# Moving the gating of the mixed rows from the gate stage into the output stage of a hybrid encoder

## The reference

```python
p = h @ w_in
..., q_mem, gate = jnp.split(p, ...)
o_mix = mla_mixer(...)            # layer 0: softmax attention; layer 1: sgu_mixer
o_mem = memory_attention(q_mem, mem, ...)
o = jnp.concatenate([o_mix, o_mem], axis=-1) * jax.nn.silu(gate)
x = x + o @ w_out[i]
```

## Time and profile before

| what | us |
|---|---|
| median of three runs | 3594.59 |
| the profiled execution, its own time | 3603.56 |
| its span, first to last instruction | 3601.5 |
| PE busy | 3326.9 (92%) |
| DVE busy | 2006.2 (56%) |
| ACT busy | 1581.8 (44%) |
| POOL busy | 1389.1 (39%) |

### The profile page before, as it was taken

The page is one execution under the profiler, slowest core; times in us unless marked ns, Lnnn a source line. Parts: engine busy times, 40 slices in busy tenths (PEclk is TensorE's granted clock), DMA queues, the critical chain, the costliest instruction groups (busy, mean ns, idle before and its releaser), DMA issues. The chain is left out here.

```text
span 3601.5 us, 46116 instructions
## 1 busy us (share of the span) xinstructions
PE 3326.9 (92%) x16108; PEld 2735.6 (76%) x16108; DVE 2006.2 (56%) x3007; ACT 1581.8 (44%) x2396; POOL 1389.1 (39%) x914
## 2 busy tenths in 40 slices
PE   8969959999999999999697998997999959799899
PEld 8968837777777777777496887885888849688787
DVE  4457758888888888888376332113333337522211
ACT  4446627777777777777454121003222225412100
POOL 1148828888888888888410000000000011000000
PEclk9979969999999999999898999998999969799999
DMA  7769980222222221221354996554222244488555
GB/s 279 260 225 314 306 233 18 66 67 61 67 62 65 52 56 44 67 61 22 115 174 129 290 292 217 197 175 177 88 91 103 90 180 165 131 259 242 175 189 173
DMA packets 454870, 537.91 MB, mean 149 GB/s; under 512 B 55609, under 2 KB 372409, under 8 KB 434993
## 3 DMA queue, kind: packets, MB, share of 16 engines
q1 hardware_dynamic: 454704, 535.81, 48.5%
HBM read 324.98 MB, written 210.61 MB: 149 GB/s over the span
## 5 line engine op out<-in xcount | busy, mean ns | idle before, releaser
L1235 POOL TENSOR_TENSOR at_acc<-at_acc,at_ph 128x1024 f32<-128x1024 f32 x288 | 690.9, 2399 | 79.0 <-ACT at_ph L1161 58.2
L1269 DVE TENSOR_TENSOR at_pl<-at_sc,at_ph 128x1024 fp32r<-128x1024 f32 x408 | 498.6, 1222 | 139.3 <-ACT at_sc L1162 139.0
L1161 ACT ACTIVATE at_ph<-at_sc 128x1024 fp32r<-128x1024 f32 x408 | 418.5, 1026 | 336.2 <-PE at_sc L1081 336.1
L1255 DVE TENSOR_REDUCE at_mx<-at_mxp 128x1 f32<-128x512 f32 x816 | 522.2, 681 | 26.7 <-PE at_mxp L1092 25.0
L1162 ACT ACTIVATE at_sc<-at_sc 128x1024 f32<-128x1024 f32 x408 | 416.3, 1020 | 0.0
L1077 PE MATMUL at_sc<-at_qt,at_kt 97*128 97x512 f32 x816 | 331.4, 406 | 12.5 <-DMA at_qt<-at_neg 9.7
L1079 PE MATMUL at_sc<-at_qt,at_kt 96*128 96x512 f32 x816 | 326.0, 399 | 0.0
L1106 PE MATMUL at_o_hi<-at_ph,at_v 128*128 128x512 f32 x816 | 322.4, 395 | 2.1 <-DVE at_half L1274 2.1
L1081 PE MATMUL at_sc<-at_qt,at_kt 96*128 96x512 f32 x816 | 323.7, 397 | 0.0
L1108 PE MATMUL at_o_lo<-at_pl,at_v 128*97 128x512 f32 x816 | 321.8, 394 | 0.0
L1092 PE MATMUL at_mxp<-at_kt,at_qt 96*128 96x512 f32 x816 | 276.8, 412 | 25.2 <-DMA at_kt<-kT 20.4
(11 more groups left out here) (246 smaller groups left out, 7350.5 us busy)
## 6 DMA issues: line engine op xcount, KB each, us to landing
ma_h<-hT SPq DMA_DIRECT2D x40, 1024.0 KB, 4.8
ogT<-ga_st SPq DMA_DIRECT2D x160, 256.0 KB, 3.5
ou_o<-ogT SPq DMA_DIRECT2D x40, 1024.0 KB, 6.1
ga_h<-hT SPq DMA_DIRECT2D x64, 512.0 KB, 7.3
hT<-lat_n_h SPq DMA_DIRECT2D x24, 1024.0 KB, 6.2
hT<-sg_n_h SPq DMA_DIRECT2D x24, 1024.0 KB, 3.8
qT<-hd_stq SPq DMA_DIRECT2D x60, 384.0 KB, 6.2
kT<-hd_stk SPq DMA_DIRECT2D x120, 192.0 KB, 3.5
```

Of the source, the lines that this page charges most:

```text
L1161: act.activation(ph[:, g], sc[g % 2][:], ACT.Exp, scale=SCALE).then_inc(p_hi, 1)
L1235: pool.tensor_tensor(acc[:, c.slot, :], f32(ph[:, (g - 1) % 4]).rearrange("p b n -> p (b n)") if t == 1 else acc[:, c.slot, :], now, ALU.a ...
L1255: dve.tensor_reduce(mx[:, n:n + 1], mxp[n % 2][:], AX.X, ALU.max).then_inc(mx_in, 1)
L1269: dve.tensor_tensor(pl[:, g], sc[g % 2][:], f32(ph[:, g]), ALU.subtract).then_inc(p_lo, 1)
```

## The change

1. The gate stage keeps only matmuls, silu and one store for each step: `sgT` (1024 x 2560 in DRAM), 256 KB, in rows of 2 KB. The loads of `omix` and `inv_s`, the products, the rounding and the subtraction leave it. The reciprocals are still made and written there, but the wait for their landing moves to the end of the stage.
2. The output stage, now `gated_output`, loads for each tile of 128 tokens the mixed rows (512 KB in pieces of 512 B), the silu (512 KB in pieces of 512 B) and, in layer 0, two broadcasts of the reciprocals (192 KB each, pieces of 512 B). DVE divides (layer 0), gates and, after ACT has rounded, subtracts. These steps for tile 0 stand ahead of the weights' rounding and split on ACT and DVE, and those for tile i+1 stand ahead of the add of tile i. The loops over tiles are written out instead of run by a register.
3. In the attention's opening on SP, the row of chunk 0 and its waits move ahead of the loads of q 2, k 1 and v 1.

```diff
                 load_q(c0.ahead(1))
                 load_v(0)
+                sp.wait_ge(const_in, 5)
+                row(c0)
                 load_q(c0.ahead(2))
                 load_k(1)
                 load_v(1)
-                sp.wait_ge(const_in, 5)
-                row(c0)
...
-def gating(nc, K, plan, following, hT, omix, ogT, name, sums=None, inv_s=None):
+def gating(nc, K, plan, following, hT, sgT, name, sums=None, inv_s=None):
...
-                    sp.wait_ge(inv_out, 16)
-                for n in range(3):
-                    load_o(n)
                 for n in range(N):
                     b, f = n // FT, n % FT
-                    if n + 3 < N:
-                        load_o(n + 3)
                     if f == 0 and b >= 1 and b + 1 < NB:
                         load_h(b + 1)
-                    sp.wait_ge(lo_in, n + 1)
-                    for a in range(2):
-                        sp.dma_start(ogT[4 * b:4 * b + 4, :, a, f * P:(f + 1) * P].rearrange(
...
+                    sp.wait_ge(sg_in, n + 1)
+                    sp.dma_start(sgT[f * P:(f + 1) * P, b * BLK:(b + 1) * BLK], sg[:, n % 3, :]
+                                 ).then_inc(out[n % 3], 16)
                 for n in range(3):
-                    sp.wait_ge(out[n], 32 * len(range(n, N, 3)))
+                    sp.wait_ge(out[n], 16 * len(range(n, N, 3)))
+                if sums is not None:
+                    sp.wait_ge(inv_out, 16)
...
                 for n in range(N):
                     act.wait_ge(mm, n + 1)
-                    if n >= 2:
-                        act.wait_ge(og_in, n - 1)
-                    act.activation(sg[:, n % 2, :], acc[n % 4][:], ACT.Silu).then_inc(sg_in, 1)
-                    if n >= 1:
-                        round_hi(n - 1)
-                round_hi(N - 1)
+                    after(act, out[n % 3], 16 * (n // 3))
+                    act.activation(sg[:, n % 3, :], acc[n % 4][:], ACT.Silu).then_inc(sg_in, 1)
...
+def gated_output(nc, K, plan, following, omix, sgT, rows_of, rows_to, name, inv_s=None):
...
+                def load_o(i):
+                    u, ts = i % 2, slice(i * P, (i + 1) * P)
+                    sp.dma_start(o[:, u], omix[:, ts].rearrange("(k p) t -> p k t", p=P)).then_inc(o_in[u], 16)
+                    sp.dma_start(sg[:, u], sgT[:, ts].rearrange("(k p) t -> p k t", p=P)).then_inc(o_in[u], 16)
+                    if inv_s is not None:
+                        for n in range(2):
+                            rows = inv_s[:, ts].rearrange("(k e) (o t) -> e o k t", e=2, o=1)[n]
+                            sp.dma_start(r[n * VH:(n + 1) * VH, u], rows.broadcast_to([VH, DIV, P])
+                                         ).then_inc(o_in[u], 16)
+
+                load_o(0)
                 w.load_rest(sp)
-                sp.dma_start(f32(o[:, 1]), ogT[1]).then_inc(o_in[1], 16)
+                load_o(1)
                 for u in range(2):
                     sp.dma_start(x[:, u, :], rows_of(u)).then_inc(x_in[u], 16)
                 w.load_following(sp)
...
+                for i in range(TILES):
+                    u = i % 2
+                    if i + 2 < TILES:
+                        sp.wait_ge(mixed, i + 1)
+                        load_o(i + 2)
                     sp.wait_ge(y_in, i + 1)
                     sp.dma_start(rows_to(i), y[:, u, :]).then_inc(y_out[u], 16)
...
+                for i in range(TILES):
+                    u = i % 2
+                    pe.wait_ge(lo_in, i + 1)
+                    after(pe, y_in, i - 1)
...
+                def round_og(i):
+                    act.wait_ge(mixed, i + 1)
+                    after(act, mm, i - 1)
+                    act.copy(og[:, i % 2, 0, :], full[:]).then_inc(hi_in, 1)
+
+                round_og(0)
                 w.round_hi(act)
+                for i in range(1, TILES):
+                    round_og(i)
...
+                def gated(i):
+                    u = i % 2
+                    dve.wait_ge(o_in[u], LOADS * (i // 2 + 1))
+                    if inv_s is not None:
+                        dve.tensor_tensor(o[:, u, 0:DIV], o[:, u, 0:DIV], r[:, u], ALU.mult
+                                          ).then_inc(divided, 1)
+                        dve.wait_ge(divided, i + 1)
+                    after(dve, lo_in, i)
+                    dve.tensor_tensor(full[:], o[:, u].rearrange("p k t -> p (k t)"),
+                                      sg[:, u].rearrange("p k t -> p (k t)"), ALU.mult).then_inc(mixed, 1)
+
+                def low(i):
+                    dve.wait_ge(hi_in, i + 1)
+                    dve.tensor_tensor(og[:, i % 2, 1, :], full[:], f32(og[:, i % 2, 0, :]), ALU.subtract
+                                      ).then_inc(lo_in, 1)
...
+                gated(0)
+                low(0)
+                w.take_lo(dve)
+                for i in range(TILES):
+                    if i + 1 < TILES:
+                        gated(i + 1)
+                        low(i + 1)
+                    add(i)
```

More of the change, by code:

```diff
@@ L1674, in gating @@
         h = s.sb("h", [P, 2, 2, KD, BLK], F32R)
[L1675 to L1680, removed]
+        sg = s.sb("sg", [P, 3, BLK])
         rows = s.sb("rows", [P, 2, NH * TOK // P])
         acc = [s.ps(f"acc{n}", [P, BLK]) for n in range(4)]
[L1683 to L1685 removed]
+        mm, sg_in, rows_in, total_in, inv_in, inv_out = (
+            s.sem(n) for n in ("mm", "sg_in", "rows_in", "total_in", "inv_in", "inv_out"))
         h_first = [s.sem(f"h_first{k}") for k in range(KD)]
         h_in = [s.sem(f"h{u}") for u in range(2)]
[L1688 removed]
         out = [s.sem(f"out{n}") for n in range(3)]
         N = NB * FT
[L1692 to L1699, removed]
         with nc.Block() as block:
@@ L1802, in _ @@
                     dve.reciprocal(rows[:, 0], rows[:, 0]).then_inc(inv_in, 1)
[L1803 to L1828, removed]
+def gated_output(nc, K, plan, following, omix, sgT, rows_of, rows_to, name, inv_s=None):
+    DIV = MIX // P
     with Space(nc, name) as s:
         w = Weights(s, plan, following)
-        o = s.sb("o", [P, 2, 2, D], F32R)
+        o = s.sb("o", [P, 2, KD, P])
+        sg = s.sb("sg", [P, 2, KD, P])
+        r = s.sb("r", [P, 2, DIV, P]) if inv_s is not None else None
+        og = s.sb("og", [P, 2, 2, D], F32R)
+        full = s.sb("full", [P, D])
         x = s.sb("x", [P, 2, D])
@@ L1839, in output @@
         y_out = [s.sem(f"y_out{u}") for u in range(2)]
+        LOADS = 64 if inv_s is not None else 32
         with nc.Block() as block:
@@ L1867, in _ @@
             def _(pe):
[L1868 to L1872, removed]
+                for i in range(TILES):
+                    u = i % 2
+                    pe.wait_ge(lo_in, i + 1)
+                    after(pe, y_in, i - 1)
                     for k in range(KD):
-                        if first and u == 0:
+                        if i == 0:
                             w.ready(pe, "o", k)
@@ L1895, in step, with add @@
+                def low(i):
+                    dve.wait_ge(hi_in, i + 1)
+                    dve.tensor_tensor(og[:, i % 2, 1, :], full[:], f32(og[:, i % 2, 0, :]), ALU.subtract
+                                      ).then_inc(lo_in, 1)
+                def add(i):
+                    u = i % 2
                     dve.wait_ge(mm, i + 1)
-                    dve.wait_ge(x_in[u], j * 16 + 16)
-                    if not first:
-                        dve.wait_ge(y_out[u], j * 16)
+                    dve.wait_ge(x_in[u], (i // 2 + 1) * 16)
+                    after(dve, y_out[u], (i // 2) * 16)
@@ L2109, in build @@
     inv_s = scratch("inv_s", [NH, TOK])
[L2110 removed]
+    sgT = scratch("sgT", [D, TOK])
     x1 = scratch("x1", [TOK, D])
@@ L2156, in build @@
             extra = dict(sums=sums, inv_s=inv_s) if layer == 0 else {}
-            gating(nc, K, *next(steps), hT, omix, ogT, f"ga{layer}", **extra)
+            gating(nc, K, *next(steps), hT, sgT, f"ga{layer}", **extra)
             src, dst = (A["x"], x1) if layer == 0 else (x1, A["y"])
-            output(nc, K, *next(steps), ogT, lambda i, src=src: tile_of(src, i),
-                   lambda i, dst=dst: tile_of(dst, i), f"ou{layer}")
+            gated_output(nc, K, *next(steps), omix, sgT, lambda i, src=src: tile_of(src, i),
+                         lambda i, dst=dst: tile_of(dst, i), f"ou{layer}", inv_s if layer == 0 else None)
 class Consts:
```

41 lines of the change are left out of this document (5 added, 36 removed).

## The result

The changed kernel takes 3604.39 us, the median of nine runs (3602.77 to 3610.88), against 3596.83 us for the kernel before in nine runs (3593.68 to 3597.90). The ratio is 1.0027, with a 95% interval of 1.0016 to 1.0037: slower by 0.27%, which is 9.7 us (5.8 to 13.3 by the interval); the medians differ by 7.6 us. The forecast was 3600.8 us, +6.2 us, in a range of 3587 to 3611.

The account below looks back on a forecast made before the run. PE was taken as the bound inside gate and output stages, so only its idle time and half clock could move. Terms -9.2 - 0.5 + 4.45 + 2.3 + 5.2 + 1.9 + 1.8 + 0.3 = +6.25 us gave 3600.8 us, range 3587 to 3611.

Parts of the forecast that it names:

- The attention's opening: Before the first attention scores: chunk 0's row no longer queues behind three loads, so scores start near 525.0, gaining 9.2 us.
- the half-clock stretch: After the first scores: 13.0 us at half clock, taken as unchanged, with -4.6 and +1 us as bounds.
- The silu's wait: Layer 0's gate stage: the first silu no longer waits for products behind the reciprocals, -0.5 us, bounds 0 and -0.6.
- The earlier first DMA: From gate to output: one store follows the last silu at once, so the output's first DMA goes 3.9 us earlier per layer.
- The hole of layer 0: Last silu to PE's output start: landing 7.6, vector steps 4.55, one split 1.2, less 5.0 and 3.9: +4.45 us.
- Tile 1 and tile 2 of layer 0: Layer 0's output: PE waits 2.3 us for tile 1 (bounds 0.8, 4) and 5.2 for tile 2 (2.5, 7.5).
- rival 1: Larger holes: slow landing, both tile waits at their slow bounds, clock falling at both; 3607 us, chance 0.16.
- landed at 2227.9: Layer 0's tile 1: its data wait for 1.05 MB of weights until some 2221.4, then last 6.1 us.
- The lost clock: Layer 0's output: the 5.2 us wait for tile 2 brings 3.8 us at half pace, losing 1.9 us.
- Layer 1's output: No weights follow and DVE has less work; tile 1 is ready about when tile 0 ends, +0.3 us.
- Later tiles: Layer 0's output: DMA needs 8.7 us of PE's 10.8 per tile, so PE stays the bound; no cost.
- The rule of the Trainium skill: Line rate from 512 B pieces: tile 0's 1.44 MB would take 3.3 us; the prediction used 6.1 from the trace.

Follow-up runs that it names:

- e1: The kernel before with only the attention's opening changed (chunk 0's row ahead of q 2, k 1 and v 1): 3588.11 us, ratio 0.9973.
- e3: The changed kernel with the spatial stage's weights issued behind tile 2's load: 3604.19 us, ratio 1.0022.
- e4: The changed kernel with the reciprocals' two broadcasts replaced by two same-size loads of distinct rows: 3606.03 us, ratio 1.0026.
- e7: The changed kernel with the reciprocals' two 64-partition loads replaced by one 384 KB load of distinct rows over 128 partitions: 3607.67 us, one execution.
- e2: The changed kernel with the attention's opening as before: 3616.22 us, ratio 1.0056.
- e8: The changed kernel without the reciprocals' loads and without the division in layer 0: 3599.61 us, one execution.

## Why the prediction was right, and where its sizes were off

The direction, the places and the sum held: +6.2 us predicted and +7.6 us measured between the medians (+9.7 by the ratio); by the stages of the profiles +7.2. That the sum held so well is in part luck: tile 1's wait came out above its bound of 4 us and tile 2's below its bound of 2.5 us, and the two errors cancel.

1. **The attention's opening: right.** Predicted -9.2 us; the stage became 9.3 us shorter, and e1 alone measures -8.3 (medians) to -9.7 us (ratio). Giving bounds to the half-clock stretch was the right way to treat it: it varies from 4.0 to 13.2 us.
2. **The silu's wait: right.** The wait of 0.5 us is gone, and layer 0's gating stage is 0.5 us shorter.
3. **The earlier first DMA: right.** Predicted 3.5 us after the last silu, measured 3.2 (2186.86 - 2183.68).
4. **The hole of layer 0: right.** Predicted 7.6 + 4.55 + 1.2 = 13.35 us from first DMA to PE, measured 13.55, of which the landing 7.7. The hole grew by 4.3 us where I had 4.45. In layer 1 it grew by 1.3 us for 1.8.
5. **Tile 1 and tile 2 of layer 0: right as a sum by luck, wrong in its parts.** I had 2.3 and 5.2 us with the clock lost at tile 2; it was 5.7 and 1.6 us with the clock lost at tile 1. By the prediction's own sign (a wait of some 3 us for tile 1) rival 1 held there, and by tile 2's wait it didn't. The step that failed is "landed at 2227.9", 10.7 us after PE's start; it was 13.9 us (2214.30 - 2200.41). That step lets only the two weights' 1.05 MB go ahead of tile 1's 1.44 MB, and puts x behind; by the count under e3 0.8 MB issued behind tile 1's load moved before tile 1 was there. At the 240 GB/s of that stretch this is 3.5 us (an estimate), about the 3.2 us that are missing, but no run moves x away from tile 1's load, so it is argued and not shown. e3 rules out the spatial weights alone. e4 leaves at most 1.0 us to the repeated reads. e7 against e4 puts about 2 us on the two loads over 64 partitions, from one execution of e7, and in it only 3.08 MB moved in the same stretch. Tile 2 was ready later than I had it, 33.8 us after PE's start (2234.23 - 2200.41) for 31.3, but PE came to it 6.0 us later than I had it, so its wait came out small.
6. **The lost clock: right that it is lost once, at the other tile.** 5.3 us at half pace after tile 1's wait (2218.91 to 2224.2) where I had 3.8 after tile 2's, so 2.6 us for 1.9.
7. **Layer 1's output: mis-sized**, +1.1 us for 0.3. It has no wait; its first 5.7 us ran at the half clock (matmuls start 0.43 us apart from 3376.30 to 3381.42), where before it was 4.0. That is chance rather than the change: the same stretch lasts 3.9 to 6.0 us in the seven variants of the changed kernel.
8. **Later tiles: right.** PE is at 100% from tile 3 on, with DMA at 0.79.

The rule of the Trainium skill that I weighed (DMA: Bandwidth & Descriptors, Specifications: line rate from pieces of 512 B on) would have given a kernel faster than before. Tile 0's 1.44 MB took 7.7 us here with its fixed part, not 4.8 (3.3 us, an estimate from the page's ceiling of 435 GB/s, and 1.5 fixed), so the measurement decides against it for these strided pieces.

The stages of e2's profile give less than its +20 us by time: +4.4 and +11.6 us in layer 0, +1.4 and +1.6 in layer 1, less 1.2 in gating, 17.8 us. But the profiled execution, 3612.60 us, is the fastest of its five and only 16.2 us above the kernel before, so the stages leave nothing unexplained. Not settled are what x behind tile 1's load costs, and whether e7's gain comes from the number of partitions or from having one DMA fewer.

The profiles before and after don't settle the forecast's +6.2 against +7.6 either: single executions of the changed kernel lie up to 8 us apart (3602.77 to 3610.88).

## What to carry to other kernels

When PE is busy for every microsecond in both stages, moving vector work from one to the other is worth nothing; what counts is the chain from a stage's first load to its first matmul, and the steps that are put in it (here a divide, a product, a rounding, a subtraction and a split: 5.8 us in layer 0) stand between the tile's landing and PE's start. Look at what a small transfer on the critical path queues behind: two lines moved on SP gave 8 to 10 us here, and they alone make the best kernel (3588 us). Where loads depend on the progress of a stage, issue the next tile's load first and the rest behind it; that took back 7 of the changed kernel's microseconds. When a sum comes out right, compare its terms too: here two wrong ones cancelled.

## What the runs showed of the hardware

- The time at the half clock after dense matmuls begin differs from one execution to another: from the first scores on it was 4.0, 4.2, 4.8, 5.4, 5.7, 10.0, 10.4 and 13.1 us in the eight profiles with the row early and 5.0 and 13.2 us in the two with the row late, with matmuls of 96 and 97 rows back to back until the clock rose. At the starts of the output stages, with matmuls of 128 rows, it was 3.0 to 6.0 us in twenty cases.
- After a wait inside dense matmuls the clock could be low at once (waits of 5.7 us in the changed kernel and 5.0 us in e4), could fall 1.4 us later (3.20 us in e7) or 0.7 us later (2.11 us in e8), or could stay high (2.75 us in e7, 3.09 us in e2).
- Bytes of DMAs that SP issued behind tile 1's load moved before tile 1 was complete: 3.33 MB moved where the two weights and the tile are 2.49 MB.
- With two DMAs of 192 KB over 64 partitions each, tile 1 was usable later than with one of 384 KB over 128 partitions in the same 512 B pieces (13.1 against 11.3 us after PE's start), in one execution each.
- Reading the same 512 B for 64 partitions costs hardly more than reading distinct rows: tile 0 was divided 7.7, 8.0 and 8.2 us after its first DMA with the broadcasts (changed kernel, e2, e3) and 8.1 us after it with distinct rows (e4).
